# Gaps of 32 to 224 bytes between the operand buffers of a two-layer macaron kernel on one Trainium2 core

## The reference

```python
for l in range(DEPTH):
    x = x + 0.5 * swiglu(rms_norm(x, ffn1_norm[l]), ffn1_w_up[l], ffn1_w_down[l])
    x = x + hybrid_mixer(rms_norm(x, mix_norm[l]), w_in[l], na_rel_bias[l], w_branch_a[l],
                         w_branch_b[l], w_out[l], pos)
    x = x + 0.5 * swiglu(rms_norm(x, ffn2_norm[l]), ffn2_w_up[l], ffn2_w_down[l])
return rms_norm(x, final_norm)
```

## Time and profile before

| | |
|---|---|
| median of 3 runs | 1195.07 us (1194.1 to 1195.33) |
| the profiled execution | 1194.9 us |
| its span, first to last instruction | 1193.0 us |
| mean granted TensorE clock | 0.998 |
| TensorE busy | 1166.7 us (98%) |
| VectorE busy | 722.3 us (61%) |
| ScalarE busy | 549.5 us (46%) |
| GpSimd busy | 71.9 us (6%) |
| HBM read | 212.89 MB |

### The profile page before, as it was taken

How to read it: one execution, slowest core, us unless ns; L and a number is a source line. 1 busy time by engine, 2 the same in 40 slices (tenths; PEclk the granted TensorE clock), 3 DMA queues, 4 the chain that set the end, 5 groups by cost and what they waited for, 6 DMA issues and landing times.

```text
span 1193.0 us, 15423 instructions
## 1 busy us (share of the span) xinstructions
PE 1166.7 (98%) x5608; PEld 963.8 (81%) x5608; DVE 722.3 (61%) x941; ACT 549.5 (46%) x694; POOL 71.9 (6%) x70
## 2 busy tenths in 40 slices
PE   4999999999999999999999999999999999999997
PEld 3888888888888888888888888888888888888885
DVE  4555556765665765555575555577557567655555
ACT  3434444555544444444454444454555435444342
POOL 1500002100200010000010000110002001000000
PEclk9999999999999999999999999999999999999999
DMA  8965556554344455565546555755433435655551
GB/s 250 270 224 188 195 195 230 180 175 140 112 155 173 145 193 194 176 205 181 194 167 211 182 179 186 272 165 188 142 129 119 159 141 176 212 187 200 177 193 36
DMA packets 146155, 214.59 MB, mean 180 GB/s; under 512 B 7617, under 2 KB 112193, under 8 KB 145857
## 3 DMA queue, kind: packets, MB, share of 16 engines
q1 hardware_dynamic: 143424, 208.50, 52.0%
q0 software_dynamic: 1920, 3.20, 1.2%
q10 hardware_dynamic: 768, 2.33, 0.7%
HBM read 212.89 MB, written 4.19 MB: 182 GB/s over the span
## 4 chain that ended last, share of the span: by engine, by line
PE 94%; DVE 2%; issue 2%; DMA 1%; ACT 0%; SPq 0%; POOLq 0%; POOL 0%; DVEq 0%; ACTq 0%
PE bank L972 29%; PE bank L974 28%; PE bank L973 28%; PE bank L1130 2%; PE bank L1036 2%; PE bank L1103 2%; PE bank L1115 1%; DMA raw<-ffn_w_up_dram 1%; PE bank L1007 1%; PE bank L1093 1%; DVE qk_raw L883 0%; DVE w_lo L681 0%; DVE qT L889 0%; ACT w_hi L489 0%; PE bank L1173 0%
## 5 line engine op out<-in xcount | busy, mean ns | idle before, releaser
L681 DVE TENSOR_TENSOR w_lo<-raw,w_hi 128x2048 fp32r<-128x2048 f32 x191 | 442.2, 2318 | 239.9 <-ACT w_hi L489 239.9
L489 ACT ACTIVATE w_hi<-raw 128x2048 fp32r<-128x2048 f32 x191 | 365.3, 1916 | 246.7 <-PE bank L974 240.2
L972 PE MATMUL bank<-w_hi,a_hi 128*128 128x512 f32 (+1 forms) x1152 | 461.4, 401 | 4.6 <-DVE w_lo L954 3.8
L974 PE MATMUL bank<-w_hi,a_lo 128*128 128x512 f32 (+1 forms) x1152 | 447.7, 389 | 0.0
L973 PE MATMUL bank<-w_lo,a_hi 128*128 128x512 f32 (+1 forms) x1152 | 446.6, 388 | 0.0
L972 PEld LDWEIGHTS bank<-w_hi,a_hi 128*128 128x128 f32 x1152 | 217.2, 189 | 50.6 <-issue 4.4
L974 PEld LDWEIGHTS bank<-w_hi,a_lo 128*128 128x128 f32 x1152 | 216.9, 188 | 45.9
L973 PEld LDWEIGHTS bank<-w_lo,a_hi 128*128 128x128 f32 x1152 | 217.6, 189 | 39.2
L972 PE MATMUL bank<-w_hi,hT_hi 128*128 128x512 f32 x352 | 137.9, 392 | 0.5 <-DVE hT_lo L769 0.5
L974 PE MATMUL bank<-w_hi,hT_lo 128*128 128x512 f32 x352 | 137.1, 389 | 0.0
L973 PE MATMUL bank<-w_lo,hT_hi 128*128 128x512 f32 x352 | 137.0, 389 | 0.0
(11 more groups left out here) (85 smaller groups left out, 641.6 us busy)
## 6 DMA issues: line engine op xcount, KB each, us to landing
raw<-ffn_w_up_dram SPq DMA_DIRECT2D x176, 512.0 KB, 4.6
raw<-w_in_dram SPq DMA_DIRECT2D x92, 512.0 KB, 4.5
raw<-ffn_w_down_dram SPq DMA_DIRECT2D x88, 512.0 KB, 3.9
raw<-w_out_dram SPq DMA_DIRECT2D x16, 512.0 KB, 3.6
raw<-w_branch_b_dram SPq DMA_DIRECT2D x8, 512.0 KB, 3.7
bias_rows<-na_rel_bias_dram POOLq DMA_DIRECT2D x24, 128.0 KB, 4.4
gain<-gains_dram SPq DMA_DIRECT2D x6, 512.0 KB, 5.5
bias<-bias_rows SPq DMA_DIRECT2D x2, 1536.0 KB, 9.2
```

Source lines behind the costliest of these rows:

```text
L489: act.activation(w_hi[slot][:, :], raw[slot][:, :], ACT.Copy).then_inc(hi_done, 1)
L681: dve.tensor_tensor(w_lo[slot][:, :], raw[slot][:, :], w_hi[slot][:, :].bitcast(F32), ALU.subtract).then_inc(lo_done, 1)
L972: pe.matmul(dst, s_hi, m_hi, start=start, stop=False)
L974: return pe.matmul(dst, s_lo, m_hi, start=False, stop=stop)
```

## The change

A helper `shifted` places a buffer so that it begins at a wanted remainder of 256 bytes (`LINE`), by taking an unused buffer ahead of it that fills the gap. `at` keeps the remainder; it begins with 128, where the first buffer lies. Nothing else is changed: no instruction, no order, no size. The weight slots get new names (`wa_hi`, `wb_hi`, `wc_hi`, `wa_lo` and so on).

```diff
+LINE = 256
+        at = [128]
+
+        def shifted(name, shape, start, dt=F32):
+
+            gap = (start - at[0]) % LINE
+            if gap:
+                sb(f"gap_before_{name}", [P, gap // 4])
+            at[0] = start
+            return sb(name, shape, dt)
         raw = [sb(f"raw{i}", [P, UNIT]) for i in range(RING)]
-        w_hi = [sb(f"w_hi{i}", [P, UNIT], F32R) for i in range(RING)]
-        w_lo = [sb(f"w_lo{i}", [P, UNIT], F32R) for i in range(RING)]
-
-        x = sb("x", [P, TT, D])
+        w_hi = [shifted(f"{s}_hi", [P, UNIT], 128 + 32 * i, F32R) for i, s in enumerate(("wa", "wb", "wc"))]
+        w_lo = [shifted(f"{s}_lo", [P, UNIT], 128 + 32 * i, F32R) for i, s in enumerate(("wa", "wb", "wc"))]
+
+        x = shifted("x", [P, TT, D], 128)
         gain = sb("gain", [P, D])
-        a_hi = sb("a_hi", [P, KT, SEQ], F32R)
-        a_lo = sb("a_lo", [P, KT, SEQ], F32R)
-        qT = sb("qT", [P, PAIRS, SEQ])
+        a_hi = shifted("a_hi", [P, KT, SEQ], 160, F32R)
+        a_lo = shifted("a_lo", [P, KT, SEQ], 224, F32R)
+        qT = shifted("qT", [P, PAIRS, SEQ], 128)
-        hT_hi = sb("hT_hi", [P, 2, SEQ], F32R)
-        hT_lo = sb("hT_lo", [P, 2, SEQ], F32R)
-        probs = sb("probs", [P, 2, TT, SEQ])
+        hT_hi = shifted("hT_hi", [P, 2, SEQ], 0, F32R)
+        hT_lo = shifted("hT_lo", [P, 2, SEQ], 32, F32R)
+        probs = shifted("probs", [P, 2, TT, SEQ], 128)
-        yT_hi = sb("yT_hi", [P, 6, SEQ], F32R)
-        yT_lo = sb("yT_lo", [P, 6, SEQ], F32R)
-        top = sb("top", [P, HEADS, TT])
+        yT_hi = shifted("yT_hi", [P, 6, SEQ], 96, F32R)
+        yT_lo = shifted("yT_lo", [P, 6, SEQ], 192, F32R)
+        top = shifted("top", [P, HEADS, TT], 128)
```

## The result

The changed kernel takes 1210.78 us (median of 4 runs, 1210.47 to 1210.94) against 1195.16 us for the kernel before in the same comparison: ratio 1.0132, 95% interval 1.0119 to 1.0146. The forecast was no change, 1195.0 us in a range of 1187 to 1205 us. The time lies outside the range, on its slow side.

The account below looks back on a forecast made before the run. TensorE was taken as the bound, through the pitch of `product`. Transfers, ScalarE and VectorE splits and 4656 products each added 0, giving 1195.0 us, range 1187 to 1205 us, with 0.70 for no change within 0.2%.

Parts of the forecast that it names:

- what bounds the kernel: TensorE, busy 1166.7 of 1193.0 us; gaps count almost only through the start-to-start pitch of `product` matmuls, 226.67 ns.
- The rest of the sum: Transfers, ScalarE's and VectorE's splits: 0 each; landings 4.6 us, splits 1916 and 2292 ns, loads 188 ns unchanged.
- C: Rival: the gaps do not arrive because the allocator moves or rounds buffers; 1195 us, chance within no change's 0.70.
- nothing to win: Matmul streaming: slope 0.4167 ns a column shows no repeated stall; at most the fixed 13.3 ns per matmul could be won.
- Rival A: TensorE's load and stream collide from equal remainders; separating them saves up to 13.3 ns on 4304 products, 1138 us; chance 0.17.
- the products ... 0 x 4656: All `product` matmuls on TensorE: address changes cost 0 for each of 4656, the load being hidden with 39 ns slack.
- the root at which it could be wrong: In `product`, pitch might depend on the weight load's remainder, which was held hidden behind the matmul before; no size or chance.
- absolute: Name used in the experiments for Rival B: a start off 64 or 128 bytes costs its own stream.
- what the kernel before shows: TensorE trace: 226.67 ns steady pitch; 230 to 340 ns after fp32 matmuls follows instruction order and should return unchanged.
- Rival B: Moving streams starting inside a memory piece take one more: slot b alone 10.2 us, 1205 us; b and c 1236 us; chance 0.13.
- Neighbours: ScalarE and VectorE working on memory cost TensorE's stream nothing: pitch stays 226.67 ns beside their splits; sum 0.

Follow-up runs that it names:

- experiment 5: Changed kernel with all weight slots at remainder 128 and all six activation buffers (`a`, `hT`, `yT`) at 192: 1216.89 us, ratio 1.0181 to the kernel before.
- Experiment 4: Changed kernel with all weight slots at remainder 128 and all six activation buffers at 160: 1216.62 us, ratio 1.0184 to the kernel before.
- experiment 1: Changed kernel with all weight slots and all six activation buffers at remainder 160: 1193.79 us, ratio 0.9993 to the kernel before.
- experiment 2: Changed kernel with all activation buffers back at remainder 128, slots a, b, c still at 128, 160, 192: 1205.21 us, ratio 1.0086 to the kernel before.
- experiment 9: Against a kernel with slots and activations all at 128, only `a_lo`, `hT_lo`, `yT_lo` moved to 160: 1215.28 us, ratio 1.0168 to the kernel before.
- experiment 3: Changed kernel with all weight slots back at remainder 128, activations left as changed: 1213.26 us, ratio 1.0155 to the kernel before.
- experiment 13: Changed kernel with all weight slots and all activation buffers at remainder 0: 1195.81 us, ratio 1.0005 to the kernel before.
- experiment 14: Changed kernel with all weight slots and all activation buffers at remainder 192: 1195.76 us, ratio 1.0007 to the kernel before.

## Why the prediction was wrong

**Right: what bounds the kernel.** Only the pitch of `product` could matter, and only it moved. The rest of the sum held: transfers 4.6 us, splits at 1918 and 2291 ns by their medians in slot b, loads at 188 ns, the waits within 0.7 us. The gaps arrived, so C is out.

**Right: nothing to win.** The slope of one column a period left no repeated stall to remove, and none was removed. Rival A does not hold: at 512 columns unequal starts never took the 13.3 ns away, and its 1138 us is near no run. At 256 columns they took up to 6.3 ns of it (experiment 5), on 96 products. The Trainium skill (TensorE: Matmul & The Clock Gate, "Back-to-back issue gap") gives by its rule an estimate of 215.8 ns for 512 columns; no kernel here had a mean settled pitch under 226.67 ns.

**Wrong: the step "the products ... 0 x 4656".** It rested on two sentences. The first was that the load touches `a`, `hT` and `yT` but has 39 ns of slack, so that its address can't matter. The load did keep its 188 ns and its slack; yet the pitch of the matmul beside it grew by 4.9 ns on average. Slack in the load's duration did not show what the load does to the stream beside it. In place of 0 for each of 4656 products the trace has 4.92 ns for each of the 3000 settled ones and 1.84 ns for some 1210 more, 17.0 us. The second was, under A, that the two streams pass each other's remainder whatever the start is, because they do not run at one speed. Experiment 4 against experiment 1 shows that the start does count: the same activations, slots 32 bytes lower, 22.8 us more. The prediction named this as the root at which it could be wrong (a pitch that depends on the remainder of the weight load), but gave it no price and no chance; the only rival on the slow side was *absolute*.

**Wrong: what the kernel before shows.** I read the clean 226.67 ns as the cost of a matmul, and the 230 to 240 ns after float32 matmuls as an affair of the order of instructions. But 226.67 ns is the pitch of products whose loads and streams start alike, reached some six to ten products after float32 matmuls; in experiment 2 slot a reached it while b and c did not. What else it could be was to be guessed at from the uneven stretch, whose mean of 230.16 ns without the first pitch is near the changed kernel's 231.60. Had the gaps kept the engine there, 3000 x (230.2 - 226.7) = 10 us or more would have been due, 1205 us and up. That is hindsight, and the likeness may be chance: that unequal starts leave the products in that same stretch is not shown. Experiments 4 and 9 are steady in their own way: in one nearly every settled product has 231 to 235 ns, in the other the same three pitches (232.5, 239.2 and 228.3 ns) come over and over.

**Rival B** had the sign and the order of size, but by luck, since its mechanism and place fail: it put 1205 us on slot b alone, the trace shows a, b and c alike (settled means 232.2, 231.6 and 231.3 ns), experiment 3 loses with no stream moved, and experiments 1, 13 and 14 lose nothing with all of them moved.

**Neighbours.** That ScalarE and VectorE cost TensorE nothing held: the settled pitch is 226.68 ns over 3000 products with VectorE busy for 61% of the time. The Trainium skill says the same (SBUF — State Buffer, "SBUF: two separate sides"). Its other statement there, that TensorE never waits for anyone, does not cover the engine's own load and stream. The Trainium skill calls the two read ports for stream and load independent (TensorE: Matmul & The Clock Gate, "Step-by-step: what each phase is for"); the runs disagree in effect, 1193.79 against 1216.62 us by nothing but where the two start.

**How the changed kernel's loss is made up.** In slot a the starts differ by +32 and +96, in slot c by -32 and +32, in slot b by 0 and +64, and by +96 and 128 for `hT` (the few products of slot c with `hT`, and those of `yT`, differ otherwise). Kept constant, all of these but 0 have a pitch of 233 to 234 ns in the table; the mix gave 231.60. The experiments don't say how a mix adds up: by *chain* it isn't the mean of its parts.

**Open.** Why equal starts give 226.67 ns and others a longer pitch is not shown: the records give starts and durations and no bank or port. Nor why -64 is mild, nor why 256 columns go the other way. Differences under 16 bytes and other sizes of product weren't run.

## What to carry to other kernels

Where TensorE is the bound and float32r products follow one another, take the distance between starts in the steadiest stretch and in an uneven one: if two levels show up, ask what holds the lower one before changing anything that touches it, addresses too. Let the loaded and the streamed operands of products begin at the same remainder of 256 bytes, all of them, upper and lower parts alike; one in three that differs loses almost the whole of it. For products of 512 columns this is shown; at 256 columns equal starts were the slower ones. A small buffer put between large ones can cost 0.5 to 2% in this way, with the same instructions, waits and clock.

## What the runs showed of the hardware that I had not expected

- The pitch of a float32r product of 128x128 by 512 columns at full clock is 226.67 ns where load and stream start alike, and 228.9 to 234.3 ns with each of seven other constant differences. The load's own duration stays at 188 ns in both.
- It is reached only after a while: after float32 matmuls the products with equal starts need six to ten starts to come down to 226.67 ns. Products with unequal starts take a longer steady pitch instead, also beside units with equal starts in the same kernel (experiment 2: 226.9, 233.4 and 229.2 ns in slots a, b and c).
- The loss is shared by neighbours: with one load in three off by 32 bytes the three pitches are 232.5, 239.2 and 228.3 ns, 700.0 ns together, as much as with all three off (experiments 9 and 4).
- At 256 columns it is the other way: 119.8 ns with equal starts, 113.6 ns with activations 64 bytes beyond the slots (experiment 5). With only 96 of these products that is 0.6 us here.
